# Nine pairs of projection tiles by seven products, an earlier first attention score, dummies and reordered router copies in a two-layer decoder step

## The reference

```
h = rms_norm(x);  z = h @ w_in            # one combined projection, 11,264 columns wide here
A: q, k normed per head; softmax attention, 3 groups of 8 heads, plus bias table; groups merged
B: gated linear attention (4 heads)      C: gated DeltaNet with a causal convolution (4 heads)
x += (sum over A, B, C of sigmoid(gate) * (mixer output @ w_branch)) @ w_out
h = rms_norm(x)
layer 0: x += (silu(h @ w_gate) * (h @ w_up)) @ w_down                  # 2816 wide
layer 1: x += top-2-of-8 experts of the same form, 1792 wide each, chosen by a router
```

## Time and profile before

| | us |
|---|---|
| median of 3 runs (lowest, highest) | 1797.36 (1794.94, 1800.5) |
| the profiled execution's own time | 1799.75 |
| its span in the trace | 1797.7 |
| busy: TensorE, VectorE, ScalarE, GpSimd | 1755.6 (98%), 743.6 (41%), 364.8 (20%), 154.3 (9%) |
| mean granted TensorE clock | 0.990 of full |

### The profile page before, as it was taken

One profiled execution on the slowest core, in us unless ns is written; L12 is line 12 of the kernel. 1 busy time (PEld: TensorE's weight loads), 2 busy tenths in 40 slices (PEclk: granted clock), 3 DMA queues, 4 the chain that ended last, 5 costly groups with the idle time before them and its releaser, 6 DMA issues.

```text
span 1797.7 us, 30187 instructions
## 1 busy us (share of the span) xinstructions
PE 1755.6 (98%) x12542; PEld 1283.8 (71%) x12542; DVE 743.6 (41%) x1548; ACT 364.8 (20%) x760; POOL 154.3 (9%) x259
## 2 busy tenths in 40 slices
PE   9999999999999999999999999999989999999997
PEld 7889888787778999978898887876853343334423
DVE  3454542435526675534644424264332332232321
ACT  2241334333101000013323343331011110100001
POOL 3000000403200111000100002042000000000000
PEclk9999999999999999999999999999979999999999
DMA  9833599999999987899536899799949999999994
GB/s 297 285 120 100 188 324 334 359 336 360 400 343 396 356 318 267 305 361 371 168 97 227 320 336 359 278 373 394 342 155 333 393 379 415 402 397 394 372 415 178
DMA packets 265852, 563.96 MB, mean 314 GB/s; under 512 B 14653, under 2 KB 163361, under 8 KB 265440
## 3 DMA queue, kind: packets, MB, share of 16 engines
q1 hardware_dynamic: 246384, 500.15, 76.3%
q0 software_dynamic: 18544, 58.58, 9.1%
q10 hardware_dynamic: 784, 3.26, 0.5%
HBM read 547.75 MB, written 196.63 MB: 414 GB/s over the span
## 4 chain that ended last, share of the span: by engine, by line
PE 83%; SPq 6%; DMA 6%; DVE 2%; issue 1%; ACT 0%; POOL 0%; DVEq 0%; ACTq 0%
PE PS L944 33%; PE PS L1604 9%; PE PS L1380 8%; SPq L815 6%; PE PS L1355 5%; PE PS L1388 4%; PE PS L863 3%; PE PS L990 3%; PE PS L1582 3%; PE PS L1370 2%; PE PS L1543 2%; PE PS L983 2%; PE PS L1642 2%; DMA out_win_p<-z 1%; PE PS L1326 1%; DMA z<-in_cache_win_kv 1%
## 5 line engine op out<-in xcount | busy, mean ns | idle before, releaser
L944 PE MATMUL PS<-h,mem 128*128 128x264 f32 x2816 | 654.6, 389 | 0.0
L944 PEld LDWEIGHTS PS<-h,mem 128*128 128x128 f32 x2816 | 527.1, 190 | 106.7 <-issue 21.8
L1812 ACT COPY z<-PS 128x264 f32<-128x264 f32 (+5 forms) x293 | 120.1, 428 | 726.9 <-PE PS L944 506.5
L1604 PE MATMUL PS<-mem,z 128*32 128x512 f32 (+1 forms) x1536 | 148.8, 530 | 3.7 <-DMA mem<-in_moe_w_up 3.1
L2899 DVE COPY small<-mem 128x1024 f32 x56 | 38.8, 693 | 182.3 <-PE PS L1582 120.8
L1604 PEld LDWEIGHTS PS<-mem,z 128*32 128x32 f32 x1536 | 47.8, 111 | 80.5 <-issue 63.8
L1355 PE MATMUL PS<-z,mem 128*128 128x264 f32 x384 | 87.3, 388 | 0.0
L1582 PE MATMUL PS<-z 128*32 128x256 f32 (+2 forms) x624 | 86.9, 396 | 0.0
L1582 PE MATMUL PS<-small,z 128*32 128x256 f32 (+2 forms) x624 | 86.9, 396 | 0.0
L1355 PEld LDWEIGHTS PS<-z,mem 128*128 128x128 f32 x384 | 72.3, 190 | 13.8 <-issue 1.7
L1380 PE MATMUL PS<-z,mem 128*128 128x132 f32 x624 | 78.6, 279 | 0.0
(11 more groups left out here) (377 smaller groups left out, 2031.7 us busy)
## 6 DMA issues: line engine op xcount, KB each, us to landing
out_win_s<-in_cache_win_kv SPq DMA_DIRECT2D x128, 1023.5 KB, 11.4
mem<-in_w_in SPq DMA_DIRECT2D x88, 1024.0 KB, 7.1
mem<-in_moe_w_gate SPq DMA_DIRECT2D x80, 512.0 KB, 10.1
mem<-in_moe_w_up SPq DMA_DIRECT2D x80, 512.0 KB, 9.2
mem<-in_moe_w_down SPq DMA_DIRECT2D x64, 512.0 KB, 14.1
out_win_s<-in_cache_win_kv SPq DMA_DIRECT2D x32, 1022.0 KB, 12.3
z<-in_moe_w_down SPq DMA_DIRECT2D x48, 512.0 KB, 13.8
z<-in_moe_w_up SPq DMA_DIRECT2D x32, 512.0 KB, 10.8
```

What stands on the lines that cost most here:

```text
L944: last = mm(bank(l, "p", j)[:, 0:T], w[:, k, P * (j % 2):P * (j % 2) + P], h[:, k, :], start=(k == 0), stop=(k == KT - 1))
L1604: last = mm(m_bank("c", "gu", g, b, w, r)[BLK * j:BLK * j + BLK, 0:n], hs[:, k, P * r + BLK * j:P * r + BLK * j + BLK], v3(slot_ap(set_slo ...
L1812: return nc.scalar.copy(out, in_)
```

## The change

- **Folded pairs.** In both layers the pairs 23, 24, 27, 28, 29, 30, 33, 35 and 37 of the projection are computed by seven products of 4 blocks by 132 columns (56 MATMUL records for a pair) in place of two tiles (32 records of 264 columns). TensorE's steps are fold_x, fold_y (full banks 0 and 1) and fold_x2, fold_y2. DVE makes three weight sums in fold_w, one chunk ahead, reduces fold_x's and fold_y's banks, adds them, and adds fold_y2's; ScalarE copies fold_x2's bank. fold_h writes four differences of h over x after tile 3. Before it SyncE stores x to x_kept ahead of load 5, and reloads it after load 42; wo waits for that. The sums lie in parts of z and the arena that are unused at their time, two small buffers move for that.
- **Attention.** Before: norm_sum.9, tiles 62 and 63, kv_tok, att_sc.0, tile 64, att_sc.1 inside 65, att_pt.0 inside 66, 67, att_pv.0, and then two tiles between steps. After: norm_sum.9, att_sc.0, tiles 62, 63, half of 64, kv_tok, rest of 64, fold_w.33, att_sc.1, 65, fold_x.33 and fold_y.33, att_pt.0, fold_x2.33 and fold_y2.33, 68, fold_w.35, att_pv.0, att_sc.2, 69, fold_x.35, fold_y.35, att_pt.1, and in the same way to att_pv.3, the last att_pt standing after one tile.
- **Bias tables.** POOL issues the first four in a step of its own, bias, after norm_sum.8, and waits there for fold_y2.29 and n4_done 7. kv_tok has the stores alone.
- **as_l and as_p** each stand one mg step later.
- **Dummies.** keep_warm(n) runs n multiplications of 128x256 into a bank that nobody reads: in layer 0 4 ahead of the last norm_part of wo, after a wait for wo's last bank, and 10 behind it; in route() 6 ahead of the wait for r_mask and 10 at its end.
- **Router copies.** find_slots(1) and weigh_slots(0) move behind bring(0, 0, 0), weigh_slots(1) behind bring(0, 1, 0).

The semaphore counts of layer 0's FFN move with the new users (hd_ready, fw_odd, fw_even), wait_z knows the new jobs, and the run tables have the new steps; those hunks are left out.

```diff
+HALF = T // 2
+UNSETTLED = ("proj", "fold_x", "fold_y", "fold_x2", "fold_y2", "fold_w")
+FOLD = (23, 24, 27, 28, 29, 30, 33, 35, 37)
...
+    def tile(j):
+        q = j // 2
+        if q not in FOLD:
+            return [("proj", j)]
...
-        return [step, ("proj_half", j), (step[0] + "2", *step[1:]), ("proj", j)]
+        first, rest = tile(j) if j // 2 in FOLD else (("proj_half", j), ("proj", j))
+        return [step, first, (step[0] + "2", *step[1:]), rest]
...
+        first, rest = tile(j) if j // 2 in FOLD else (("proj_half", j), ("proj", j))
+        return [first, *steps, rest]
...
     for n in range(7, 10):
-        s += p() + [("norm_sq", n)] + p() + [("norm_sum", n)]
-    s += p()
-    s += p(64 - 21 - 18 - 16 - 8) + [("kv_tok",), ("att_sc", 0)] + p() + between(("att_sc", 1)) + between(("att_pt", 0)) + p() + [("att_pv", 0)]
-    for t in range(1, AH // 2):
-        s += [("att_sc", t + 1)] * (t + 1 < AH // 2) + p(2) + [("att_pt", t)] + p(2) + [("att_pv", t)]
+        s += p() + [("norm_sq", n)] + p() + [("norm_sum", n)] + [("bias",)] * (n == 8)
+    s += [("att_sc", 0)] + p(2) + between(("kv_tok",))
+    for t in range(AH // 2):
+        s += [("att_sc", t + 1)] * (t + 1 < AH // 2) + p(2 if t < AH // 2 - 1 else 1) + [("att_pt", t)] + p(2) + [("att_pv", t)]
     s += [("bar", 0), ("as_t",)] + between(("as_q", 0), ("sig", 0))
     for m in range(1, 8):
         s += [("as_q", m)] + [("sig", m)] * (m < 2) + p()
-    s += [("sig", 2), ("as_l",), ("mg", 1, 0), ("mg", 1, 1), ("as_p",), ("mg", 1, 2), ("mg", 1, 3), ("as_v", 0)]
+    s += [("sig", 2), ("mg", 1, 0), ("as_l",), ("mg", 1, 1), ("mg", 1, 2), ("as_p",), ("mg", 1, 3), ("as_v", 0)]
     s += [("mg", 2, 0), ("mg", 2, 1), ("mg", 2, 2), ("as_v", 1), ("as_o",), ("mg", 2, 3)]
     s += [("mg", 0, q) for q in range(4)] + [("bar", 1), ("wo",)]
     assert next(proj, None) is None
+    s.insert(s.index(("proj", 3)) + 1, ("fold_h",))
+    for q in FOLD:
+        before = ("fold_y", q - 1) if q - 1 in FOLD else ("proj", 2 * q - 2)
+        s.insert(s.index(before) + 1, ("fold_w", q))
     return s
...
-                place(n0 + q, q % RING, (l, "p", 2 * q + 1))
+                place(n0 + q, q % RING, (l, "fold_y2", q) if q in FOLD else (l, "p", 2 * q + 1))
...
+        def fold_set(q):
+            if q > 30:
+                return S_G0 if q == 37 else S_G1
+            return (S_G0 if q == 30 else S_LA if q >= Z_K // 2 else S_K0) + q % 2
...
+        def fold_quarters(l, q):
+            w = v3(chunk(CH0[l] + q), KT)
+            return w[:, 0:4, 0:P], w[:, 4:8, 0:P], w[:, 0:4, P:2 * P], w[:, 4:8, P:2 * P]
...
+                    if n == RING:
+                        sp.wait_ge(sems["h_ready"], V("h_ready", l, KT - 1))
+                        sp.dma_start(x_kept[l], x_flat).then_inc(x_in, 16)
                     load(CH0[l] + n, source(l, n))
+                    if n == FOLD[-1] + RING:
+                        wait_full(sp, l, "fold_y2", FOLD[-1])
+                        sp.wait_ge(x_in, 64 + 32 * l)
+                        sp.dma_start(x_flat, x_kept[l]).then_inc(x_in, 16)
                     shift_some(l, n)
             assert not pieces
             for name in ("bar_v", "bar_a", "bar_p"):
...
+            def keep_warm(n, out):
+                for _ in range(n):
+                    mm(out[:, 0:2 * P], ident, con[:, 0:2 * P], start=True, stop=True)
...
+            def four(out, left, right, opens=False):
+                for k in range(4):
+                    last = mm(out, left[:, k, :], right[:, k, :], start=(opens and k == 0), stop=(k == 3), skip_group_check=True)
+                return last
+            def fold_x(l, q):
+                wait_chunk(pe, CH0[l] + q)
+                open_bank(pe, l, "fold_x", q)
+                x_ = bank(l, "fold_x", q)
+                four(x_[:, 0:HALF], fold_quarters(l, q)[0], h[:, 0:4, 0:HALF], True)
+                pe.wait_ge(hd_ready, h_sum(l, 3))
+                pe.wait_ge(fw_even, even_sum(l, q, 1))
+                four(x_[:, HALF:T], fold_sums(q)[1], fold_t[:, 1]).then_inc(full(l, "fold_x", q), 1)
+            def fold_y(l, q):
+                pe.wait_ge(fw_odd, odd_sum(l, q))
+                open_bank(pe, l, "fold_y", q)
+                y_ = bank(l, "fold_y", q)
+                four(y_[:, 0:HALF], fold_sums(q)[0], fold_t[:, 0], True)
+                four(y_[:, HALF:T], fold_quarters(l, q)[2], fold_t[:, 2]).then_inc(full(l, "fold_y", q), 1)
+            def fold_x2(l, q):
+                open_bank(pe, l, "fold_x2", q)
+                four(bank(l, "fold_x2", q)[:, 0:HALF], fold_quarters(l, q)[1], h[:, 4:8, 0:HALF]).then_inc(
+                    full(l, "fold_x2", q), 1)
+            def fold_y2(l, q):
+                open_bank(pe, l, "fold_y2", q)
+                y_ = bank(l, "fold_y2", q)
+                four(y_[:, HALF:T], fold_quarters(l, q)[3], fold_t[:, 3])
+                pe.wait_ge(fw_even, even_sum(l, q, 2))
+                four(y_[:, 0:HALF], fold_sums(q)[2], h[:, 4:8, HALF:T]).then_inc(full(l, "fold_y2", q), 1)
             def conv_s(l):
                 pe.wait_ge(convt_in, 16 * (l + 1))
                 open_bank(pe, l, "cs")
...
+                if t == 0:
+                    pe.wait_ge(sems["n4_done"], V("n4_done", l, 8))
                 for i in range(TT):
                     n = P * (i + 1)
                     for r in range(1 + i):
...
                     last.then_inc(full(l, "wo", d), 1)
                     if d:
                         norm_part(l, 1, d - 1)
+                if l == 0:
+                    wait_read(pe, l, "wo", KT - 1)
+                    keep_warm(4, bank(l, "wo", KT - 1))
                 norm_part(l, 1, KT - 1)
+                if l == 0:
+                    keep_warm(10, bank(l, "wo", KT - 1))
             def product(out, left, right, opens=False):
...
+                keep_warm(6, bank(1, "rl", 0))
                 pe.wait_ge(r_mask, 1)
                 open_bank(pe, 1, "rc", 0)
...
                 last.then_inc(full(1, "rp", 0), 1)
+                keep_warm(10, bank(1, "rl", 0))
             def token_rows(n):
...
+            def fold_x2(l, q):
+                wait_full(act, l, "fold_x2", q)
+                copy(fold_out(q)[:, 0:HALF], bank(l, "fold_x2", q)[:, 0:HALF]).then_inc(free(l, "fold_x2", q), 1)
...
+            def fold_h(l):
+                dve.wait_ge(x_in, 64 + 32 * l)
+                h11, h12, h21, h22 = h[:, 0:4, 0:HALF], h[:, 0:4, HALF:T], h[:, 4:8, 0:HALF], h[:, 4:8, HALF:T]
+                tt(fold_t[:, 0], h12, h11, SUB)
+                tt(fold_t[:, 2], h22, h12, SUB).then_inc(hd_ready, 1)
+                dve.wait_ge(hd_ready, h_sum(l, 1))
+                tt(fold_t[:, 1], h22, fold_t[:, 0], SUB).then_inc(hd_ready, 1)
+                dve.wait_ge(hd_ready, h_sum(l, 2))
+                tt(fold_t[:, 3], h21, fold_t[:, 1], SUB).then_inc(hd_ready, 1)
...
+            def fold_w(l, q):
+                wait_chunk(dve, CH0[l] + q)
+                if fold_before(q) is not None:
+                    wait_full(dve, l, "fold_y2", fold_before(q))
...
+                a11, a12, a21, a22 = fold_quarters(l, q)
+                s1, s2, s4 = fold_sums(q)
+                tt(s1, a21, a22, ADD)
+                tt(a21, a11, a21, SUB).then_inc(fw_odd, 1)
+                dve.wait_ge(fw_odd, odd_sum(l, q))
+                tt(s2, a22, a21, SUB).then_inc(fw_even, 1)
+                dve.wait_ge(fw_even, even_sum(l, q, 1))
+                tt(s4, a12, s2, SUB).then_inc(fw_even, 1)
+            def fold_x(l, q):
+                if q != FOLD[0]:
+                    wait_read(dve, l, "fold_y2", FOLD[FOLD.index(q) - 1])
+                wait_full(dve, l, "fold_x", q)
+                nc.vector.tensor_reduce(fold_ve[:, 0, :], bank(l, "fold_x", q)[:, 0:T].rearrange("p (w t) -> p t w", w=2),
+                                        AX.X, ADD).then_inc(free(l, "fold_x", q), 1)
+            def fold_y(l, q):
+                wait_full(dve, l, "fold_y", q)
+                nc.vector.tensor_reduce(fold_ve[:, 1, :], bank(l, "fold_y", q)[:, 0:T].rearrange("p (w t) -> p t w", w=2),
+                                        AX.X, ADD).then_inc(free(l, "fold_y", q), 1)
+                wait_read(dve, l, "fold_x", q)
+                wait_read(dve, l, "fold_y", q)
+                tt(fold_out(q)[:, 3 * HALF:4 * HALF], fold_ve[:, 0, :], fold_ve[:, 1, :], ADD)
+            def fold_y2(l, q):
+                wait_full(dve, l, "fold_y2", q)
+                tt(v3(fold_out(q)[:, HALF:3 * HALF], 2), v3(bank(l, "fold_y2", q)[:, 0:T], 2),
+                   bc(fold_ve[:, 0, :], 1, [P, 2, HALF]), ADD).then_inc(free(l, "fold_y2", q), 1)
...
+                dve.wait_ge(x_in, 80 + 32 * l)
                 for d in range(KT):
...
-                find_slots(1)
-                for g in range(2):
-                    weigh_slots(g)
```

(11 more changed lines are left out.)

95 lines of the change are left out of this document (67 added, 28 removed).

## The result

The changed kernel takes 1801.03 us (median of 20 runs, 1798.15 to 1808.42), the kernel before in 20 runs beside it 1795.43 (1792.3 to 1808.91): ratio 1.0032, 95% interval 1.0020 to 1.0044. It is slower by 0.3%; 1790 was forecast, with a range from 1774 to 1802. One run of the kernel before in a later group took 2018.41 us at a mean clock of 0.846, and no figure here includes it.

A forecast was written before the change was run, and what follows sets the result against it. TensorE's work and its 42 us idle were taken as the bound, expert-weight DMA setting the end. Terms 15.1 + 7 + 10.2 - 17.8 - 2.6 - 4.3 = 7.6 faster: 1790 against the median of 1797.36, range 1774 to 1802.

The forecast's parts named there:

- Attention, what goes: At att_sc.1 and att_pt.0, today's loss behind waits for stored keys disappears in both layers: 10.2 us gained.
- (b): At att_pt.0, TensorE still waits for late key stores and the work behind them: -1.9 and -2.9, together -4.8 us.
- Half clock behind the waits, -2.6: After (a), TensorE's clock may fall: 1.3 us lost a layer, between 0 and 3.4.
- (a): Before half of tile 64, TensorE waits 2.8 us a layer for ScalarE's copy of tile 62 behind att_sc.0's exponentials: -5.6.
- slower rival: Clock falls behind four waits, (a) and fold_h's in both layers, 3.4 us each, and router dummies fail: 1810; chance 0.10.
- +7 for the router: In the router, dummies keep the gather at full clock, so SyncE's first reload and the end come 7.0 us earlier.
- Folds, +15.1: In the projection, a folded pair takes 6.30 us instead of 7.14; 0.84 x 18 pairs gains 15.1.
- (c): In attention, fold_x2.35 and .37 wait for ScalarE's copy behind the next exponentials: -1.45 four times, -5.8 us.
- (d): At eight places of attention, DVE reads banks in place of ScalarE, 0.2 us each as a hand-over: -1.6.
- fold_h, -4.3: At each layer's start, fold_h waits for stored x and delays copies behind it: -2.8 us in layer 1, -1.5 in layer 0.
- FFN start and as_l, 0: Layer 0's FFN dummies cost what they save (bounds -2 and +2 us); moving as_l trades one DVE wait for another: 0.
- 31 less 1 to 4 of remnants: Rival that attention's and x_kept's new waits are hidden, 31 us gained less remnants: 1768 to 1782; chance 0.20.

The follow-up runs named there:

- r4: Changed kernel with only the six pairs ahead of attention folded and attention in its old order: 1789.57 us, ratio 0.9970.
- r13: r10 with the first four bias tables issued in kv_tok again, ahead of the key stores: 1779.57 us, ratio 0.9926.
- r10: Changed kernel with six folds, old attention order, fold_h behind tile 14, key stores before value stores, no dummies at layer 0's wo: 1779.83 us, ratio 0.9910.
- r9: The kernel before, unchanged, run again for a second profiled execution: ratio 1.0009 to itself, profiled span 1789.7 us.
- r1: Changed kernel without the router's 6 and 10 dummies, early copies kept: 1800.00 us, ratio 1.0027.
- r11: r10 without the router's 16 dummies too: 1780.45 us, ratio 0.9902.
- r8: Changed kernel with pairs 35 and 37 not folded in either layer, order kept: 1793.47 us, ratio 0.9991.
- r7: Changed kernel without the 4 and 10 dummies at layer 0's wo and without their bank wait: 1797.19 us, ratio 1.0019.
- r14: r10 with as_l and as_p one mg step earlier, as in the kernel before: 1778.18 us, ratio 0.9914.

## Why the prediction was wrong

Three steps failed: what the kernel would win at att_pt.0, how much half clock follows the new waits, and the base.

**Attention, what goes and (b).** The prediction let all 10.2 of the old loss at the stored keys go and put -4.8 in its place. In the run TensorE stands 3.0 and 3.8 at att_pt.0 and runs att_pt.0 partly slow; 6.5 and 7.2 pass from the end of fold_y.33 to the end of att_pt.0's turn, against 2.0 of work, so 9.7 for both layers, nearly the bound of 10.2. TensorE's idle time there was 2.4 and 4.3 before, 6.7 in all, and is 6.8 now. The term "what goes" was therefore mostly a loss that stayed. Two things made it so. The first is "8.2 by proportion", which gave 9 to 10 from kv_tok's end to the last key's landing. It came 11.0 and 11.7 after kv_tok's end, and 8.9 and 9.9 after its own issue. Bytes of tables were reckoned as queued ahead of the keys, but they hardly delay them: in r4, with no tables ahead, the last keys took 12.4 and 14.5 from their issue, against 10.5 and 13.2 before, and r13 differs from r10 by nothing that can be told. Why the changed kernel's keys landed faster than r4's stays open. The second is the cover, the work of TensorE between kv_tok and att_pt.0, which had shrunk from 13.2 us (2.1 + 3.6 + 1.8 + 2.1 + 1.8 + 1.8) to 11.1. I counted the new cover and never the old one. The keys landed 1.4 and 3.3 sooner, counted from kv_tok's end, than before (12.4 and 15.0), and TensorE arrived 2.1 sooner. r4, which takes back the order and the three folds in attention, is 11 faster than the changed kernel.

**Half clock behind the waits, -2.6.** Too small: 1.7 behind (a) in each layer, 2.2 and some 0.9 behind (b), and 1.7 behind fold_h's wait in layer 1, 8.2 in this execution. The slower rival had this mechanism, at 3.4 for each of four waits; it came at half of that, behind three of them.

**The base.** One profiled execution was taken for the kernel, and its distance of 2.4 from a median of three was called spread. With 20 runs the distance is 4.3, while the changed kernel's profile lies 0.5 under its median; that makes 4.9. r9 shows one source: half clock in the router, 66.1 us there against 59.7. The +7 for the router was right to 0.2 against the first profile (7.2), 0.8 against r9's, and nothing that the median shows (r1, r11). By the clocks of the 90 runs the long half clock may come in about half of them, which would leave about half of the 7. Where a clock below full level explains a stretch of the one profile, its gain has to be multiplied with how often that comes; the clocks and times of three runs were too few to see it.

**Folds, +15.1.** Measured 0.765 a pair on the six pairs ahead of attention, 13.8 if it holds for all 18: the size was 9% high. The Trainium skill's 81 ns for 128 columns ("TensorE: Matmul & The Clock Gate", "Back-to-back issue gap"), from which the prediction worked out a loss of some 40, is not borne out: a record of 132 columns took 6.41 / 56 = 0.1145 us, 2.6% over half of a record of 264.

**Attention, (a), (c) and (d).** (a) 2.8 was 2.65 in both layers, (c) 1.45 was 1.46 four times, both with the releaser named. (d), 1.6, shows only as the 0.2 beside each wait of (c) in r8, and is not measured by itself.

**fold_h, -4.3.** Layer 1's start lost 4.7, layer 0's nothing (x_kept landed at 38.5, TensorE did not wait). In layer 1 the wait was the 2.8 of the forecast, in part by luck: x_kept took 15.9 to land and not 13.1, but TensorE went on 4.4 after that, where the forecast had 6.4. The rest is mostly the half clock above. So the sum was right, its parts were not.

**FFN start and as_l, 0.** Within their bounds: 2.4 lost before the FFN, 3.2 won in it; undoing them (r7, r14) gave differences that the intervals don't tell from none.

Against the profiled execution that gives: -7.6 forecast, +0.7 measured, 8.3 apart. 4.9 for (b), 5.6 for half clock and 1.3 for the folds make 11.8. From that go 1.3 for fold_h without its half clock (3.0 against 4.3), 1.6 for (d), and 0.8, 0.3 and 0.2 for the FFN's start, (a) and the router: 7.6 are accounted for, 0.7 are not. Another 4.9 lie between the two profiles' difference (+0.7) and the medians' (+5.6): the base.

One sum among the rivals does not come out: 31 less 1 to 4 of remnants gives 1767 to 1770 from the median of 1797.36, not 1768 to 1782; no row gives the upper end.
